# w_down of each expert loaded in blocks of two row tiles of all 1024 columns, in place of blocks of all row tiles of 512 columns

## The reference

```python
def expert_choice_moe(h, router_w, w_gate, w_up, w_down):
    ...
    gate, idx = lax.top_k(aff.T, cap)
    xs = tok[idx]
    hid = jax.nn.silu(jnp.einsum('ecd,edf->ecf', xs, w_gate)) * jnp.einsum('ecd,edf->ecf', xs, w_up)
    ye = jnp.einsum('ecf,efd->ecd', hid, w_down) * gate[..., None].astype(h.dtype)
    out = jnp.zeros_like(tok).at[idx.reshape(-1)].add(ye.reshape(-1, D))
    return out.reshape(B, L, D)
```

## Time and profile before

| | |
|---|---|
| Time, median of 3 runs | 1520.48 us (1520.21 to 1521.71) |
| The profiled execution's own time | 1519.86 us |
| Its span, first to last instruction | 1518.1 us |
| PE busy | 1455.9 us (96%) |
| DVE busy | 1186.7 us (78%) |
| ACT busy | 816.4 us (54%) |
| DMA queue of SyncE | 213468 packets, 361.13 MB |
| All DMA packets | 220745, 387.97 MB |

### The profile page before, as it was taken

How to read it: one execution, slowest core, us unless ns; L and a number is a source line. 1 busy time by engine, 2 the same in 40 slices (tenths; PEclk the granted TensorE clock), 3 DMA queues, 4 the chain that set the end, 5 groups by cost and what they waited for, 6 DMA issues and landing times.

```text
span 1518.1 us, 18595 instructions
## 1 busy us (share of the span) xinstructions
PE 1455.9 (96%) x6886; PEld 1219.8 (80%) x6886; DVE 1186.7 (78%) x1002; ACT 816.4 (54%) x760; POOL 169.0 (11%) x121
## 2 busy tenths in 40 slices
PE   7999999999999999994799999999999999999994
PEld 6788888877788888883688888888888888888883
DVE  5688988995657676326688888888888888888887
ACT  6322332213622222323477777778777777777775
POOL 1000001000005200010102121012110121101110
PEclk9999999999999999997899999999999999999997
DMA  7110323522362345638899999999999999999995
GB/s 232 56 42 17 92 59 136 173 88 84 103 233 88 113 165 201 230 148 314 299 369 373 378 375 372 385 375 377 374 377 381 377 375 374 382 376 377 374 372 209
DMA packets 220745, 387.97 MB, mean 256 GB/s; under 512 B 8571, under 2 KB 87483, under 8 KB 220188
## 3 DMA queue, kind: packets, MB, share of 16 engines
q1 hardware_dynamic: 213468, 361.13, 66.9%
q0 software_dynamic: 7232, 26.22, 5.7%
HBM read 348.52 MB, written 38.80 MB: 255 GB/s over the span
## 4 chain that ended last, share of the span: by engine, by line
PE 50%; DVE 1%; DMA 0%; ACT 0%; issue 0%; POOLq 0%; POOL 0%
PE ps L1644 16%; PE ps L1646 16%; PE ps L1645 16%; PE ps L1975 1%; PE ps L1969 1%; DVE final_rows L1600 1%; DMA slot_tokens<-tok_rows,rows_to_gather 0%; DVE expert_lo L1136 0%; ACT expert_hi L787 0%; POOLq L83 0%; DVE expert_out L1611 0%; DVE expert_out L1618 0%; DVE slot_tokens_T_lo L1136 0%; ACT slot_tokens_T_hi L787 0%; ACT L1114 0%
## 5 line engine op out<-in xcount | busy, mean ns | idle before, releaser
L1136 DVE TENSOR_TENSOR expert_lo<-expert_raw,expert_hi 128x2048 fp32r<-128x2048 f32 (+1 forms) x288 | 604.1, 2112 | 95.4 <-ACT expert_hi L787 94.2
L787 ACT ACTIVATE expert_hi<-expert_raw 128x2048 fp32r<-128x2048 f32 (+1 forms) x288 | 511.4, 1777 | 180.9 <-PE ps L1646 177.2
L1644 PE MATMUL ps<-expert_hi,slot_tokens_T_hi 128*128 128x512 f32 (+1 forms) x768 | 290.4, 378 | 3.0 <-DVE slot_tokens_T_lo L1136 2.4
L1645 PE MATMUL ps<-expert_lo,slot_tokens_T_hi 128*128 128x512 f32 (+1 forms) x768 | 285.8, 372 | 0.0
L1646 PE MATMUL ps<-expert_hi,slot_tokens_T_lo 128*128 128x512 f32 (+1 forms) x768 | 285.7, 372 | 0.0
L1644 PE MATMUL ps<-hT_hi,w_hi 128*128 128x512 f32 x576 | 227.5, 395 | 0.9 <-DVE hT_lo L1148 0.9
L1646 PE MATMUL ps<-hT_hi,w_lo 128*128 128x512 f32 x576 | 224.3, 389 | 0.0
L1645 PE MATMUL ps<-hT_lo,w_hi 128*128 128x512 f32 x576 | 224.2, 389 | 0.0
L1644 PEld LDWEIGHTS ps<-expert_hi,slot_tokens_T_hi 128*128 128x128 f32 x768 | 144.5, 188 | 26.4 <-issue 3.7
L1646 PEld LDWEIGHTS ps<-expert_hi,slot_tokens_T_lo 128*128 128x128 f32 x768 | 144.6, 188 | 20.4
L1170 DVE SCALAR_TENSOR_TENSOR conv_sum<-a_padded,small_params,conv_sum 128x1024 f32<-128x1024 f32 x120 | 158.1, 1317 | 3.4
(11 more groups left out here) (269 smaller groups left out, 1786.1 us busy)
## 6 DMA issues: line engine op xcount, KB each, us to landing
expert_raw<-in_w_gate SPq DMA_DIRECT2D x64, 1024.0 KB, 9.0
expert_raw<-in_w_up SPq DMA_DIRECT2D x64, 1024.0 KB, 9.6
expert_raw<-in_w_down SPq DMA_DIRECT2D x64, 1024.0 KB, 8.1
expert_raw<-in_w_gate SPq DMA_DIRECT2D x32, 768.0 KB, 6.9
expert_raw<-in_w_up SPq DMA_DIRECT2D x32, 768.0 KB, 6.9
expert_raw<-in_w_down SPq DMA_DIRECT2D x32, 768.0 KB, 9.0
w_raw<-in_w_in SPq DMA_DIRECT2D x36, 512.0 KB, 4.8
gate_in<-gate_spill SPq DMA_DIRECT2D x22, 512.0 KB, 3.8
```

Source lines behind the costliest of these rows:

```text
L787: nc.scalar.activation(out, src, ACT.Copy, **scale).then_inc(s, 1)
L1136: V.tensor_tensor(out, src, high_part.bitcast(F32), ALU.subtract).then_inc(s, 1)
L1644: nc.tensor.matmul(out, a[0], b[0], start=first, stop=False)
L1645: nc.tensor.matmul(out, a[0], b[1], start=False, stop=False)
```

## The change

A w_down block now holds two row tiles and all 1024 columns, so that each row read from memory is 4 KB. Chunks 0 and 1 have two such blocks, of the same size as before. Chunk 2, with three row tiles, has one block of two row tiles (1 MB) and one of one row tile (512 KB), where it had two of 768 KB. In the slot a row tile lies as two places of 512 columns. TensorE runs over the row tiles and for each of them over the two halves of the columns, so it changes the bank after every three matmuls and has both halves complete only with the second block. What waited for the first half alone, `gate_out` and `late_half`, now waits for both blocks.

```diff
--- before.py
+++ after.py
@@ -390,7 +390,7 @@
         GU_UNITS = [(kind, c, kh) for c in range(NF) for kh in range(2) for kind in ("gate", "up")]
 
         def down_units(c):
-            return [("down", c, dh) for dh in range(2)]
+            return [("down", c, th) for th in range(2)]
 
         def gu_units(c):
             return [u for u in GU_UNITS if u[1] == c]
@@ -401,20 +401,24 @@
         LEAD = len(gu_units(0))
         SKIPPED = len(down_units(2))
 
+        def down_tiles(c, th):
+
+            return list(range(2 * th, min(2 * th + 2, FC[c][1] // P)))
+
         def src_of(kind, c, k, e):
 
             a, n = FC[c]
             if kind == "down":
-                tiles = n // P
-                return w_down[bass.ds(e, 1), a:a + n, k * 512:(k + 1) * 512].rearrange(
-                    "o (t p) n -> p (o t) n", p=P), tiles, 512
+                tiles = down_tiles(c, k)
+                return w_down[bass.ds(e, 1), a + tiles[0] * P:a + (tiles[-1] + 1) * P, :].rearrange(
+                    "o (t p) n -> p (o t) n", p=P)
             w = w_gate if kind == "gate" else w_up
             return w[bass.ds(e, 1), k * 4 * P:(k + 1) * 4 * P, a:a + n].rearrange(
-                "o (t p) n -> p (o t) n", p=P), 4, n
+                "o (t p) n -> p (o t) n", p=P)
 
         def place_of(kind, c, k):
-            a, n = FC[c]
-            return (n // P, 512) if kind == "down" else (4, n)
+
+            return (2 * len(down_tiles(c, k)), 512) if kind == "down" else (4, FC[c][1])
 
         FIRST = [n for n in range(NB) if not LEAD <= n < LEAD + SKIPPED]
         assert NB % RAWS == 0 and NB % SPLITS == 0
@@ -457,8 +461,10 @@
             kind, c, k = BODY[n]
             owner = e - 1 if (kind, c) == ("down", 2) else e
             tiles, width = place_of(kind, c, k)
-            src, _, _ = src_of(kind, c, k, owner)
-            sp.dma_start(EW[count % RAWS][:, 0:tiles, 0:width], src).then_inc(e_landed[count % RAWS], 16)
+            place = EW[count % RAWS][:, 0:tiles, 0:width]
+            if kind == "down":
+                place = place.rearrange("p (t h) n -> p t (h n)", h=2)
+            sp.dma_start(place, src_of(kind, c, k, owner)).then_inc(e_landed[count % RAWS], 16)
 
 
         @block.sync
@@ -1028,7 +1034,7 @@
 
             def split_e(n, e, base):
 
-                r, (tiles, width) = slot_of(n, e), place_of(*BODY[n][:2], 0)
+                r, (tiles, width) = slot_of(n, e), place_of(*BODY[n])
                 act.wait_ge(e_landed[r], landed_of(n, e))
                 ge(act, e_used, base + pos(n, e) - SPLITS + 1)
                 q = pos_mod(n, e, SPLITS)
@@ -1055,7 +1061,7 @@
 
                 for dh in range(2):
                     act.wait_ge(slots_ready, 2)
-                    act.wait_ge(e_used, used + dh)
+                    act.wait_ge(e_used, used + 1)
                     ge(act, added, e * 16)
                     out = nc.scalar.activation(YE[:, dh * 512:(dh + 1) * 512], PS[:, 4 + dh, :], ACT.Copy,
                                                scale=GATES[:, bass.ds(e, 1)])
@@ -1104,7 +1110,7 @@
                 count = base + q
                 act.wait_ge(e_landed[count % RAWS], 16 * (count // RAWS + 1))
                 act.wait_ge(e_used, count - SPLITS + 1)
-                tiles = FC[2][1] // P
+                tiles, _ = place_of("down", 2, q)
                 high(ES[count % SPLITS][:, 0:tiles, :], EW[count % RAWS][:, 0:tiles, :], e_hi)
             final_square(1)
             hidT_high(2, E - 1, base)
@@ -1604,7 +1610,7 @@
                 V.tensor_scalar(RSTDF[:, t:t + 1], SUMSQF[:, t:t + 1], 1.0 / D, 1e-6, ALU.mult, ALU.add).then_inc(var_ready, 1)
 
             def late_half(dh):
-                dve.wait_ge(e_used, base + dh + 1)
+                dve.wait_ge(e_used, base + 2)
                 dve.wait_ge(rows_back, 16)
                 dve.wait_ge(slots_ready, 2)
                 part = slice(dh * 512, (dh + 1) * 512)
@@ -1992,20 +1998,22 @@
                     mm.then_inc(e_used, 1)
 
             def down(c, e, counts):
-                tiles = FC[c][1] // P
+                last = FC[c][1] // P - 1
                 pe.wait_ge(hidT_lo, NF * e + c + 1)
                 if c == 0:
                     ge(pe, ye_ready, e)
-                for dh in range(2):
-                    count, q, r = counts[dh]
+                for th in range(2):
+                    count, q, r = counts[th]
                     pe.wait_ge(e_lo, count + 1)
-                    for t in range(tiles):
-                        mm = product(PS[:, 4 + dh, :], (HIDT[0][:, t, :], HIDT[1][:, t, :]),
-                                     (ES[q][:, t, :], EL[r][:, t, :]), c == 0 and t == 0, c == NF - 1 and t == tiles - 1)
+                    for place, t in enumerate(down_tiles(c, th)):
+                        for dh in range(2):
+                            mm = product(PS[:, 4 + dh, :], (HIDT[0][:, t, :], HIDT[1][:, t, :]),
+                                         (ES[q][:, 2 * place + dh, :], EL[r][:, 2 * place + dh, :]),
+                                         c == 0 and t == 0, c == NF - 1 and t == last)
                     mm.then_inc(e_used, 1)
 
             def down_counts(c, e, base):
-                ns = [BODY.index(("down", c, dh)) for dh in range(2)]
+                ns = [BODY.index(("down", c, th)) for th in range(2)]
                 return [(base + pos(n, e), pos_mod(n, e, SPLITS), slot_of(n, e)) for n in ns]
 
             def pe_body(e, base, first, last):
```

## The result

The changed kernel takes 1523.49 us (median of 20 runs, 1521.72 to 1525.63), the kernel before beside it 1521.47 us (median of 20, 1519.54 to 1522.80). The ratio is 1.0016, 95% interval 1.0010 to 1.0022: 2.4 us slower by the ratio (1.5 to 3.3), with medians 2.0 us apart; small but clear of zero, and inside the 0.2% that were named.

A forecast was written before the change was run, and what follows sets the result against it. TensorE was taken to bound the experts, with loads covered by a 10 us lead. Loads 0, matmuls 0, preparation 0.3 and tail 2.0 gave +2.3 us, 1522.8 us; range 1520.4 to 1525.2.

The forecast's parts named there:

- The loads: w_down loads with 4 KB rows: up to 1.4 us per expert faster, worth 0 on the time.
- SyncE waits for TensorE again: Profile sign, 1000 to 1100 us: SyncE waits several us for TensorE in place of 0.3.
- DMA's share: Profile sign among the experts: the DMA engines' mean busy share falls below 1.05.
- TensorE: w_down matmuls changing output bank after every three: same count and steps, cost 0.
- Preparation: ScalarE's weight block preparation in the experts, released later by chunk 2's larger first block: +0.3 us in all.
- G2: Second block of chunk 1, released later: ready 0.03 us in time where it had 0.5 us more.
- The tail: End of kernel: late rows' first half waits for both blocks, starts 1.95 to 2.11 us later; +2.0 us.
- (B): Rival: the 0.03 us margin fails, stalls of 0.1 to 0.2 us in 15 experts, 1524 to 1525.5 us; chance 0.22.
- (A): The forecast itself, preparation stalls up to 0.06 us per expert, 1522.4 to 1523.4 us; chance 0.58.
- (C): Rival: the tail's delay is absorbed by stores or scatters behind VectorE, 1520.5 to 1521 us; chance 0.10.
- (D): Rival: w_down loads pace the experts, 4 KB rows save up to 0.5 us each, 1515 us; chance 0.04.
- (E): Rival: loads get slower from mixed sizes or longer rows; 1537 us at 10% slower; chance 0.06.

The follow-up runs named there:

- experiment 4: Changed kernel with the same blocks laid in their slots by column halves, so rows move as 2 KB again; 1523.60 us, ratio 1.0017 to the kernel before.
- experiments 3: Changed kernel with the last expert's two chunk 2 blocks multiplied by column halves again, late_half(0) waiting for the first nine matmuls only; 1521.64 us, ratio 1.0000.
- the first pair of 5: 48-column ScalarE copy ahead of the wait for the buffer of chunk 1's second block; kernel before 1521.11 us (0.9997), changed kernel 1523.79 us (1.0013).
- Experiment 5: 48-column ScalarE copy per expert, finally behind the buffer wait of chunk 1's second block; kernel before 1521.68 us (1.0003), changed kernel 1525.35 us (1.0026).
- experiments 1 to 3: Tail runs: the tail's wait alone in the kernel before, 1.0012; changed kernel with VectorE's tail queue reordered, 1.0006; changed kernel with last blocks by halves, 1.0000.
- experiment 1: Kernel before with one edit: the late rows' first half also waits for the second w_down block; 1523.34 us, ratio 1.0012.

## Why the prediction was right

**The loads: right on the time, too high on the gain.** Their price of 0 is shown by experiment 4. The period of the loads came down by at least 48.62 - 47.78 = 0.84 us per expert, since they keep pace with TensorE, and the packets' time by 1.1 us per expert, 0.9 of it by the rows' length alone. That is less than the 1.4 that I took. It is more than the estimate of 0.4 from the overhead per packet that the Trainium skill states ("DMA: Bandwidth & Descriptors", Why small descriptors are slow); the measurement decides. SyncE waits for TensorE again, as said. DMA's share did not fall below 1.05, so it was no sign of whether the loads have room: it is 1.05 at 377 GB/s, where they lag behind TensorE, and at 384, where they keep up. That three loads in flight fill the share at either pace would explain it, but no run varies their number.

**TensorE: right.** Averaged over 12 experts of either trace and counted from the token transposes, the starts of the matmuls of w_down's blocks of chunks 0, 1 and 2, in turn over two banks, stand within 0.015 us of those of before or keep the distance that they came with.

**Preparation: right in place, low in size; the mechanism is shown in part.** The forecast starts came to 0.01 us. In those averages the starts up to G2's second matmul agree to 0.015 us, G2's own to 0.002; over G2's next ten they fall back by 0.034 us and stay there, and 0.009 come in chunk 2's gate and up blocks. The drift at the same ten starts is there in the traces of three other kernels with the changed experts (experiments 3, 4 and the first pair of 5), two of which also list two or three short waits for a low half, 0.3 and 0.5 us in all. The term was 0.02 x 15 = 0.3 us and measured 0.5 us on average (0.7 in this pair). Experiment 5 shows that the slack is spent; that the drift itself would go with more slack is argued from its place and not shown. That the loss comes as slightly longer steps and not as a wait in the rows is told below; why 0.009 us are lost in chunk 2 stays open.

**The tail: right.** The start of the late rows' first half was forecast 1.95 to 2.11 us later, and 2.0 us taken as the cost. Counted from the start of TensorE's last matmul it came 1.95 us later (from 1.52 ahead of it to 0.43 behind), and VectorE's idle time and the end are 1.89 us, in the place named, and by experiments 1 to 3 it is the wait's, through what is queued behind it. GpSimd and SyncE's stores covered nothing.

**The sum.** That +2.3 came so near to +2.4 is partly luck: the preparation was taken 0.2 us too low and the tail 0.1 too high, and the interval of the measured difference, 1.5 to 3.3 us, could not have told these apart. The 1522.8 us was 0.7 us low, because its base of three runs was 1.0 us low.

**The rivals.** (B), 0.1 us and more at G2, came true only with the added copy. Between it and (A) lie a few hundredths of a us per expert, and only the traces tell them apart. (C), an absorbed tail, is out by experiment 1. (D), loads that set the pace, is out with 18 slots by experiment 4, and true with 9. (E), slower loads, did not come: the 1 MB loads of w_down land in 7.7 us (median) in place of 8.1. The new 512 KB ones take 10.0 us where the 768 KB ones took 9.0, but with 18 slots no split waits for a landing.

## What to carry to other kernels

Whoever makes the pieces of a stream unequal moves two times for each of them, when its buffer is released and when its successor is wanted, and has to check every block behind it for both; half a microsecond of slack was the whole margin here, and the reverse order of the same two blocks cost 7 us more. A transfer that is made more efficient pays only where its lead runs out: compare the period of the loads with that of the engine that uses them, and the lead with their difference times the rounds. Here 0.9 us a round was covered by 18 slots and not by 9. At the end of a kernel a wait costs what stands in the queue behind it, so an operation that got a later input should be moved behind work that needs nothing new.

## What the runs showed of the hardware

After a pause TensorE's starts are further apart for a while. Timeline of TensorE in the kernel before, behind token transposes:

```profile
1010.56 0.39 PE L1645 MATMUL ps<-expert_lo,hidden_T_hi 128*128 128x512 f32 x1
...
1012.64 0.39 PE L1645 MATMUL ps<-expert_lo,hidden_T_hi 128*128 128x512 f32 x1
...
1013.32 0.39 PE L1645 MATMUL ps<-expert_lo,hidden_T_hi 128*128 128x512 f32 x1
...
1015.36 0.39 PE L1645 MATMUL ps<-expert_lo,hidden_T_hi 128*128 128x512 f32 x1
```

Nine steps take 2.08 us right behind the transposes and 2.04 us a little later, 0.231 and 0.227 us each, at the same granted clock of 1.00. G2 in the changed kernel shows the like: no wait in the rows, but ten starts that are 0.003 us further apart each. So a block that is ready at the last moment seems to cost a few hundredths of a microsecond even where no wait is listed; that its late readiness is the cause is the likely reading, not shown by a run of its own. In the changed kernel, with the copy of experiment 5, 0.15 us of delay cost 0.10 us of period on top of this.
